# Another order, and another rounding, of the on-chip tiles of a three-block layer kernel

## Time and profile before

| | us |
|---|---|
| median of three runs | 3368.56 |
| lowest and highest | 3368.26, 3371.16 |
| the profiled execution, device time | 3368.26 |
| its span, first to last instruction | 3366.5 |
| busy: TensorE, VectorE, GpSimd, ScalarE | 2923.8, 1404.1, 1152.8, 963.4 |
| mean granted TensorE clock | 0.915 of full speed |

### The profile page before, as it was taken

The page is one execution under the profiler, slowest core; times in us unless marked ns, Lnnn a source line. Parts: engine busy times, 40 slices in busy tenths (PEclk is TensorE's granted clock), DMA queues, the critical chain, the costliest instruction groups (busy, mean ns, idle before and its releaser), DMA issues. The chain is left out here.

```text
span 3366.5 us, 39336 instructions
## 1 busy us (share of the span) xinstructions
PE 2923.8 (87%) x16452; PEld 2378.8 (71%) x16452; DVE 1404.1 (42%) x1728; ACT 963.4 (29%) x1282; POOL 1152.8 (34%) x502
## 2 busy tenths in 40 slices
PE   7999999769999999999999989956356698998677
PEld 6888768758888877788888878844225576896455
DVE  4333384444334485542442138356763342003353
ACT  3322331133223244632433222121201322221231
POOL 3444334004444446444444434420000133445012
PEclk9999999869999999999999999977566799999888
DMA  3333220002333222232333233310302223222002
GB/s 137 99 98 103 92 70 27 3 17 90 98 95 104 96 88 75 82 97 91 94 94 100 94 106 97 97 44 7 32 13 37 74 87 101 89 93 69 0 25 75
DMA packets 91463, 251.83 MB, mean 75 GB/s; under 512 B 33440, under 2 KB 34592, under 8 KB 90400
## 3 DMA queue, kind: packets, MB, share of 16 engines
q1 hardware_dynamic: 82080, 247.32, 24.0%
q10 hardware_dynamic: 9216, 2.10, 0.4%
HBM read 240.74 MB, written 6.29 MB: 73 GB/s over the span
## 5 line engine op out<-in xcount | busy, mean ns | idle before, releaser
L438 POOL TENSOR_TENSOR weight_ring_r<-weight_ring,weight_hi_r 128x1024 fp32r<-128x1024 f32 (+2 forms) x412 | 1034.4, 2511 | 1664.7 <-ACT weight_hi_r L431 1664.7
L431 ACT ACTIVATE weight_hi_r<-weight_ring 128x1024 fp32r<-128x1024 f32 (+2 forms) x412 | 448.5, 1089 | 1605.9 <-PE acc L638 1249.9
L636 PE MATMUL acc<-p_r,weight_hi_r 128*128 128x512 f32 x1680 | 657.9, 392 | 19.6 <-POOL weight_ring_r L438 13.0
L638 PE MATMUL acc<-p_r,weight_ring_r 128*128 128x512 f32 x1680 | 655.6, 390 | 0.0
L637 PE MATMUL acc<-scr_r,weight_hi_r 128*128 128x512 f32 x1120 | 437.2, 390 | 0.0
L636 PEld LDWEIGHTS acc<-p_r,weight_hi_r 128*128 128x128 f32 x1680 | 316.9, 189 | 87.0 <-POOL weight_ring_r L438 20.0
L638 PEld LDWEIGHTS acc<-p_r,weight_ring_r 128*128 128x128 f32 x1680 | 316.6, 188 | 66.0
L637 PE MATMUL acc<-p_r,weight_hi_r 128*128 128x512 f32 x888 | 345.9, 390 | 0.0
L636 PE MATMUL acc<-scr_r,weight_hi_r 128*128 128x512 f32 x768 | 308.3, 401 | 15.6 <-DVE p_r L657 10.4
L638 PE MATMUL acc<-scr_r,weight_ring_r 128*128 128x512 f32 x768 | 300.6, 391 | 0.0
L637 PE MATMUL acc<-h_r,weight_hi_r 128*128 128x512 f32 x696 | 273.3, 393 | 0.0
(11 more groups left out here) (524 smaller groups left out, 4215.4 us busy)
## 6 DMA issues: line engine op xcount, KB each, us to landing
weight_ring<-in_weights SPq DMA_DIRECT2D x372, 512.0 KB, 3.5
weight_ring<-in_weights SPq DMA_DIRECT2D x32, 704.0 KB, 4.0
weight_ring<-in_weights SPq DMA_DIRECT2D x8, 640.0 KB, 3.8
x<-in_x SPq DMA_DIRECT2D x4, 512.0 KB, 7.8
lift<-h SPq DMA_DIRECT2D x1, 2048.0 KB, 8.7
p<-lift SPq DMA_DIRECT2D x8, 256.0 KB, 11.4
p<-lift SPq DMA_DIRECT2D x1, 2048.0 KB, 8.7
out<-x SPq DMA_DIRECT2D x1, 2048.0 KB, 7.2
```

The source lines that it names most:

```text
L431: self.nc.scalar.activation(self.r.weight_hi[:, ahead, 0:width], self.weight_ring[:, r, 0:width], ACT.Copy)\
L438: self.nc.gpsimd.tensor_tensor(rest, raw, hi, ALU.subtract).then_inc(self.weights_split, 1)
L636: pe.matmul(out, hi, op.hi(kx), start=kx == 0, stop=False)
L638: mm = pe.matmul(out, lo, op.hi(kx), start=False, stop=sub == g.q - 1 and k == g.kc - 1)
```

## The change

The tiles `x`, `h`, `p`, `weight_ring` and `weight_hi` keep their order. Behind them the order becomes `vec`, `cst`, `eye`, `ones`, `rstd`, `scr`, `small` where it was `scr`, `rstd`, `eye`, `ones`, `small`, `cst`, `vec`, and the start and all sizes are rounded up to multiples of 32 bytes where it was 64. Nothing else is changed; the instructions are the same, in the same order, with other addresses.

```diff
--- before.py
+++ after.py
@@ -333,11 +333,11 @@
             p=[P, 52, T],
             weight_ring=[P, RING, SLOT],
             weight_hi=[P, AHEAD, SLOT],
-            scr=[P, 8, T], rstd=[P, T], eye=[P, P], ones=[P, P], small=[P, 256],
+            vec=[P, N_VEC],
             cst=[P, 3980],
-            vec=[P, N_VEC])
-
-        self.r, at = Rounded(), -(-nc.sbuf_base // 64) * 64
+            eye=[P, P], ones=[P, P], rstd=[P, T], scr=[P, 8, T], small=[P, 256])
+
+        self.r, at = Rounded(), -(-nc.sbuf_base // 32) * 32
         place, alias = {}, {}
         for name, shape in shapes.items():
             place[name] = nc.alloc_sbuf_tensor_at(name, shape, F32, offset=at)
@@ -345,8 +345,8 @@
                 alias[name] = nc.alloc_sbuf_tensor_at(f"{name}_r", shape, F32R, offset=at)
             elif name in ("h", "p", "scr"):
                 alias[name] = Chunks([nc.alloc_sbuf_tensor_at(f"{name}_r{c}", [P, T], F32R, offset=at + 4 * T * c) for c in range(shape[1])])
-            at += -(-4 * int(np.prod(shape[1:])) // 64) * 64
-        self.x, self.h, self.p, self.weight_ring, self.weight_hi, self.scr, self.rstd, self.eye, self.ones, self.small, self.cst, self.vec = place.values()
+            at += -(-4 * int(np.prod(shape[1:])) // 32) * 32
+        self.x, self.h, self.p, self.weight_ring, self.weight_hi, self.vec, self.cst, self.eye, self.ones, self.rstd, self.scr, self.small = place.values()
         self.r.h, self.r.p, self.r.weight_ring, self.r.weight_hi, self.r.cst, self.r.scr = (
             alias[n] for n in ("h", "p", "weight_ring", "weight_hi", "cst", "scr"))
         self.acc = ctx.enter_context(nc.psum_tensor("acc", [P, BANKS, T], F32))
```

## The result

| | before | after |
|---|---|---|
| median of four runs, us | 3368.89 | 3398.94 |
| lowest and highest | 3368.26, 3371.16 | 3396.83, 3402.47 |
| profiled execution, device time | 3368.26 | 3400.84 |
| its span | 3366.5 | 3399.0 |

The ratio is 1.0089, with a 95% interval from 1.0072 to 1.0106: the change makes the kernel 30 us slower. The forecast was no measurable change, and 3398.9 is above the upper end of its range, 3378.

What follows compares the result with a forecast made beforehand. It took the dense matmuls' pitch to bound most of the kernel, and VectorE, ScalarE and waits some 400 us. All terms were 0: 3368.26 + 0 = 3368.3, forecast as 3368.5 us, range 3363 to 3378.

Steps and rivals of the forecast that it cites:

- TensorE, moving operand: Dense matmuls streaming scratch from 32 B past a multiple of 64: bounds 0 and 7.1 ns a matmul, taken as 0.
- the slower rival: 3,312 rounded matmuls streaming scratch pay 7.1 ns each for its start, 23.5 us in all, so 3392; chance 0.10.
- All stay multiples of 32, so nothing changes below that size: Starts of the moved tiles: all remain multiples of 32 B, leaving only starts 32 past 64 and place as questions.
- The price of 0 for VectorE, ScalarE, GpSimd and DMA: Their accesses to moved tiles cost nothing more; upper bounds +4.5 us for VectorE, +4.8 us for DMA.
- The faster rival: L657's splits quicken as scratch leaves the buffers GpSimd and ScalarE work on: -10.4 us, so 3358; chance 0.08.
- What the profile after would show: Signs: if right, L637 within 1 ns of 389, 882 matmuls from 200 to 400 us; contrary signs for each rival.

Runs made afterwards that it cites:

- b1: Kernel before without its layers, TensorE alone in groups of 72 dense matmuls differing in operand starts: 226.7 ns a matmul at equal starts, 233.3 with the stationary 32 B beyond.
- e2: Kernel before with 32 B gaps ahead of scratch and of rstd, moving scratch alone off multiples of 64: 3398.49 us, ratio 1.0091.
- e3: Kernel before with a 32 B gap ahead of the first tile, so that all tiles move together: 3367.72 us, ratio 0.9998.
- e1: Changed kernel's tile order, but start and sizes rounded up to 64 B as in the kernel before: 3394.17 us, ratio 1.0077 to the kernel before.
- e9: Kernel after, its order and rounding to 32 kept, with a 96 B gap ahead of scratch: 3368.38 us, ratio 0.9997 to the kernel before.
- e11: Kernel before with gaps of 192 B ahead of the weight ring and 64 B ahead of scratch: 3388.97 us, ratio 1.0059.
- e6: Kernel before with 128 B gaps ahead of the weight ring and ahead of scratch: 3421.84 us, ratio 1.0160.
- e10: Kernel before with gaps of 160 B ahead of the weight ring and 96 B ahead of scratch: 3423.99 us, ratio 1.0163.
- e8: Kernel before with gaps of 480 B ahead of the weight ring and 32 B ahead of scratch: 3422.99 us, ratio 1.0163.
- e4: Kernel before with 32 B gaps ahead of the weight ring and ahead of scratch: 3423.72 us, ratio 1.0167.
- e5: Kernel before with 64 B gaps ahead of the weight ring and ahead of scratch: 3404.76 us, ratio 1.0109.
- b2: Kernel before without its layers, TensorE alone in groups of 48 matmuls over finer operand distances: 226.7 ns a matmul at distance 0, none of the finer ones quicker.

## Why the prediction was wrong

**The step that failed** is "TensorE, moving operand", the dense stream of 512 columns, priced at 0. Measured, it is 30.0 us (3398.94 - 3368.89), all of it there. The 3,312 matmuls of the slower rival carry 9.1 ns each by that, above its 7.1; but they don't carry it alone. Scratch is an operand of 768 + 1,120 triples of L636 to L638 and of 320 of L528 with 512 columns, 2,208 triples or 6,624 matmuls. The timeline shows the whole triple slower. Two starts of L636 that lie six matmuls apart, before:

```profile
2099.71 0.39 PE L636 MATMUL acc<-scr_r,weight_hi_r 128*128 128x512 f32 x1
...
2101.07 0.39 PE L636 MATMUL acc<-scr_r,weight_hi_r 128*128 128x512 f32 x1
```

and after, where the middle one of a triple streams the unmoved h:

```profile
2099.89 0.39 PE L636 MATMUL acc<-scr_r,weight_hi_r 128*128 128x512 f32 x1
2100.12 0.39 PE L637 MATMUL acc<-h_r,weight_hi_r 128*128 128x512 f32 x1
2100.36 0.39 PE L638 MATMUL acc<-scr_r,weight_ring_r 128*128 128x512 f32 x1
...
2101.28 0.39 PE L636 MATMUL acc<-scr_r,weight_hi_r 128*128 128x512 f32 x1
```

1.36 us became 1.39 us for six, so about 5 ns a matmul (starts are given to 10 ns, so 2 to 8). b1 has the two patterns of such a triple by themselves, with one or with two of three streams moved by 32 B (L3606, L3608): 231.1 - 226.8 = 4.3 ns a matmul in both. 6,624 x 4.3 = 28.5 us, against 30.0 measured, whose interval is 24 to 36 us; the product by tokens gave back 1.7 us (its first group runs for 90.2 us after, 91.9 before). The distance in these patterns is 224, which is that of e2 and not the 96 of the kernel after; b1 has 96 only for all matmuls of a group, where it costs 7.4 ns for 6.5 at 224.

**Why the argument for 0 failed.** It compared the streamed start with a grid of 64 B, and asked of each operand alone whether it costs more there. The relation between two operands of one matmul never came up, though every number for it could be worked out: all operands of the dense products share phase 128 before, and scratch is 160 B beyond it after. The rows that I took as evidence couldn't have shown it. L3126 and L3125 stream 64 columns, one of them strided, and L2661's and L2673's loads are those of other small matmuls; the earlier trace rows has nothing whose pace is set by 512 streamed columns beside a load. In the kernel after, too, they are as they were or quicker (L2661's loads 192 ns, L3125 405, L3126's median 393 where it was 404). "All stay multiples of 32, so nothing changes below that size" was true, and left out that something may change above it.

**The slower rival** had the place and the sign right, and its price of 23.5 us (3392) was near. Its mechanism, a stream that opens one more 64 B piece, was wrong: e3 has 32 beyond the grid everywhere and costs nothing, and e1 has nothing beyond it and costs 26 us. At a chance of 0.10 it was far too low for a form that no row showed, on the engine that sets the time: the bound was known, and only rows of other forms stood against it.

**What held.** The price of 0 for VectorE, ScalarE, GpSimd and DMA: e9 has constants and rstd 32 past a multiple of 64, and its time is that of the kernel before. Groups on VectorE after, columns as in the earlier trace rows, where L2599 was 686 ns, L2602 684 and L657 3,023:

```profile
L2599 DVE TENSOR_TENSOR p<-p,cst 128x512 f32<-128x512 f32 x16 | 10.0, 688 | 0.1
...
L2602 DVE TENSOR_TENSOR p<-p 128x512 f32<-128x512 f32 x16 | 10.0, 688 | 0.0
...
L657 DVE SCALAR_TENSOR_TENSOR scr_r<-x,vec,h_r 128x512 fp32r<-128x512 f32 x8 | 24.2, 3024 | 11.4 <-ACT h_r L648 11.4
```

L2602, on p alone, has the same 2 to 4 ns more as L2599 with the moved mask, so the start isn't what they come from. Copies into scratch still land in 2.4 us, and L3125 waited for them for 6.2 us (7.7 in the earlier trace rows). The faster rival fell by L657: scratch lies 20 KB further, and the 3,023 ns are 3,024. By the Trainium skill's port rule (SBUF — State Buffer, "Who interferes with whom") that is what should come; the trace agrees, and e9, with all moved tiles at or near their new places, gives 0.9997.

**What the profile after would show** was set out well enough: of the signs named for the slower rival both came, L637 with scratch above L637 with p, and fewer matmuls in a dense window. What wasn't foreseen is that an unmoved tile in the same triple, h, shows it as well.

**Sizes that the pitch explains.** The 512-column products have (2,704 + 576) x 3 = 9,840 matmuls. At distance 192 b1's 2.2 ns would make 21.6 us, and e11 measured 20.5, though its two runs lie 11 us apart and its interval is 13 to 27 us; at 128 its 5.6 ns would make 55 us, e6 measured 55.0; at 160 and at 224 its 6.5 ns would make 64, and e10 measured 55.5, e8 56.2. Part of these 8 us was idle time taken up: in e10's profile TensorE is busy for 2983.5 us of 3419.3 where it was 2923.8 of 3366.5, so busy 59.7 us longer and idle 6.9 us less. The rest stays open. In e4 and e5 scratch had a distance of its own (224, 192), and e5's lower price fits the cheap distance 192 for its scratch part; this was only argued.

**What stays open** is the inner mechanism: why a phase modulo 256 B between the stream and the loads counts, why 240, 252 and 192 are cheap or free and 4 is not (240 had 226.7 ns in b1 and 228.5 in b2, so single groups can't be told apart below some 2 ns), and why a phase that changes from one matmul to the next costs even where the two operands of each agree (L3614, 232.1 ns). I tried the pairing of a stream with its own stationary operand (L3614), with the one loaded for the next matmul (L3616), and the other order (L3618): none gets back to 226.8.

## What to carry to other kernels

Where TensorE sets the time with dense matmuls, give all operand tiles of them, streamed and stationary, the same start modulo 256 B, by padding each size, and the chunks inside it, to a multiple of 256; here up to 1.7% hung on it, and 96 B of gap repaired it. When addresses move, work out the starts relative to one another and not only against a grid. And a form that isn't in the trace, on the engine that sets the time, deserves a chance that fits its bound, whatever rows of other forms say.

## What the runs showed of the hardware that was not expected

- The pitch of rounded matmuls of 128 x 128 x 512 depends on the starts of their operands: 226.7 to 227.5 ns at distances 0, 252 and 256 B, 226.7 and 228.5 at 240, 229.0 at 192, and 230.7 to 234.2 at the others of b1.
- The durations of the matmul records grow with it by a few ns of their 389 (396 at the median of L3582 in b1, 394 in L637 after), and those of the loads don't (187 to 188 ns): what it costs is to be read from starts, or from counts in a busy window.
- A streamed start 4 B beyond that of the kernel before costs 11 ns a matmul by itself; one 32 or 128 B beyond doesn't, at distance 0.
- With 256 columns the sign turns: 119.7 ns at distance 0 and 117.9 at 64. In the kernel this shows in the one product by tokens, 768 matmuls of L528, which stream the weights against h and scratch as stationary operands. Its group with the low part of the weights and scratch has a mean of 280 ns where the earlier trace rows has 283:

```profile
L528 PE MATMUL acc<-weight_ring_r,scr_r 128*128 128x256 f32 x256 | 71.6, 280 | 0.0
```

- At distance 64 the same product gains more. Before, its first group runs from 2903.2 to 2995.1 us, 765 pitches of 120.1 ns; in e11 (weights 192 beyond the rest) it takes 86.8 us, 113.5 ns a pitch, and in e5 (distances 64 and 192) as long:

```profile
L530 PE MATMUL acc<-weight_hi_r,scr_r x256: 276/276/356, 2920.8 to 3007.6; 128*128 128x256 f32 x128
```

So a layout with distance 0 in the wide products and 64 in this one might beat the kernel before by some 5 us (an estimate, 91.9 less 86.8; no run has it). Why b1 has 117.9 ns at that distance and not 113.5 stays open.
